# All index keys ahead of the index queries, and tiles 2 to 4 admitted in one piece

## What is computed

```
z = xn @ w_in
u, q, k, v, qi, ki, wi = jnp.split(z, cuts, axis=-1)
...
s = jnp.einsum('bthd,bsd->bths', qi, ki) * (IDX_DIM ** -0.5)
score = jnp.einsum('bths,bth->bts', jax.nn.relu(s), wi)
score = jnp.where(kpos[None, None, :] <= qpos[None, :, None], score, -jnp.inf)
_, sel = lax.top_k(score, topk)            # topk = 256
...
s = jnp.einsum('btkgd,btnkd->btkgn', qg, ksel) * (HEAD_DIM ** -0.5)
s = jnp.where(valid[:, :, None, None, :], s, -jnp.inf)
p = jax.nn.softmax(s, axis=-1)
o = jnp.einsum('btkgn,btnkd->btkgd', p, vsel)
```

## Time and profile before

| | |
|---|---|
| time, median of 3 runs | 1186.83 us (1186.34 to 1189.43) |
| profiled execution | 1187.31 us, span 1185.5 us, mean granted clock .959 |
| TensorE busy | 1076.1 us (91%) |
| VectorE busy | 563.1 us (47%) |
| ScalarE busy | 414.2 us (35%) |
| GpSimd busy | 232.7 us (20%) |

### The profile page before, as it was taken

The page is one execution under the profiler, slowest core; times in us unless marked ns, Lnnn a source line. Parts: engine busy times, 40 slices in busy tenths (PEclk is TensorE's granted clock), DMA queues, the critical chain, the costliest instruction groups (busy, mean ns, idle before and its releaser), DMA issues. The chain is left out here.

```text
span 1185.5 us, 16400 instructions
## 1 busy us (share of the span) xinstructions
PE 1076.1 (91%) x6212; PEld 731.3 (62%) x6212; DVE 563.1 (47%) x1275; ACT 414.2 (35%) x976; POOL 232.7 (20%) x270
## 2 busy tenths in 40 slices
PE   4999999999996888999999898599999999999980
PEld 2555443454453666777788556378787878787860
DVE  3124568999998777766851362212211111111114
ACT  1234446667644244455562234211111111111114
POOL 1433134554420000000040210012121212122110
PEclk9999999999996899999999899789999999999995
DMA  6510000010082211101111752399999999999928
GB/s 222 204 47 12 6 28 1 1 36 6 27 227 76 107 54 54 54 19 54 37 54 63 285 230 72 129 336 356 313 345 338 344 329 347 332 341 341 290 31 311
DMA packets 51198, 191.42 MB, mean 161 GB/s; under 512 B 10910, under 2 KB 13806, under 8 KB 40885
## 3 DMA queue, kind: packets, MB, share of 16 engines
q1 hardware_dynamic: 39439, 142.71, 34.0%
q0 software_dynamic: 11536, 47.71, 14.2%
q10 hardware_dynamic: 158, 0.16, 0.1%
HBM read 162.49 MB, written 28.19 MB: 161 GB/s over the span
## 5 line engine op out<-in xcount | busy, mean ns | idle before, releaser
L1500 PEld LDWEIGHTS ps<-mem 128*128 128x128 f32 x2048 | 236.9, 194 | 16.7 <-issue 16.7
L1576 ACT ACTIVATE mem<-ps 128x512 f32<-128x512 f32 (+8 forms) x342 | 150.8, 484 | 247.1 <-PE ps L1298 63.0
L1500 PE MATMUL ps<-mem 128*128 128x96 f32 x2048 | 236.3, 277 | 0.8 <-DVE mem L2481 0.8
L2049 DVE TENSOR_SCALAR_CACHE_REDUCE mem<-mem 128x768 bf16<-128x768 f32 (+2 forms) x134 | 166.5, 1283 | 0.0
L1341 PE MATMUL ps<-mem 128*128 128x256 f32 (+1 forms) x544 | 126.3, 385 | 4.5 <-DVE mem L2347 3.5
L1506 PE MATMUL ps<-mem 128*96 128x512 f32 x256 | 117.6, 602 | 2.5 <-DVE mem L2473 2.5
L1341 PEld LDWEIGHTS ps<-mem 128*128 128x128 f32 (+1 forms) x544 | 100.6, 190 | 20.8 <-DVE mem L2347 5.6
L2473 DVE TENSOR_TENSOR mem<-mem,ps 128x192 f32<-128x192 f32 x32 | 11.4, 355 | 213.2 <-ACT mem L1925 213.2
L1002 POOL DMA_INDIRECT h_rows<-mem x32 | 46.5, 1454 | 296.4 <-DVE mem L2488 287.2
L1925 ACT ACTIVATE mem<-ps 128x192 f32<-128x192 f32 x32 | 10.6, 332 | 262.8 <-PE ps L1500 262.8
L1506 PEld LDWEIGHTS ps<-mem 128*96 128x96 f32 x256 | 39.1, 162 | 57.1 <-issue 51.2
(11 more groups left out here) (303 smaller groups left out, 1396.1 us busy)
## 6 DMA issues: line engine op xcount, KB each, us to landing
mem<-in_expert_w_gate SPq DMA_DIRECT2D x32, 1024.0 KB, 5.2
mem<-in_expert_w_up SPq DMA_DIRECT2D x32, 1024.0 KB, 8.8
mem<-in_expert_w_down SPq DMA_DIRECT2D x32, 1024.0 KB, 13.3
mem<-in_x_prompt SPq DMA_DIRECT2D x16, 512.0 KB, 4.1
mem<-in_w_in SPq DMA_DIRECT2D x3, 2048.0 KB, 10.9
h_rows<-mem SPq DMA_DIRECT2D x8, 512.0 KB, 2.6
xn_rows<-mem SPq DMA_DIRECT2D x8, 512.0 KB, 2.8
mem<-h_rows SPq DMA_DIRECT2D x8, 512.0 KB, 5.9
```

Of the source, the lines that this page charges most:

```text
L1500: ins = mm(ps[:, 2 + s, j * CAP:(j + 1) * CAP], wgu[w][:, j // 2, k, (j % 2) * P:(j % 2 + 1) * P], xgT[:, s, k, :], start=(k == 0), stop=( ...
L1576: return fn(out, in_, ACT.Copy, scale=scale)
L2049: v.tensor_scalar(bufs[a % 3][0:R, 0:w], sc, mid[:, a:a + 1], None, ALU.is_ge, ALU.add, accum_out=cnt[:, a:a + 1]).then_inc(step, 1)
```

## The change

There are two parts. In phase 1 the keys of all nine tiles come first, then the index queries, in the order `ASKING = [7, 6, 5, 4, 3, 2, NT]`; those of tiles 0 and 1, which no selection reads, are left out. And the admission of tiles 2 to 4 is done by VectorE in one piece ahead of the copies of the samples' scores, not in phase 2b; `PIECES` stays as it is.

```diff
+ASKING = [7, 6, 5, 4, 3, 2, NT]
...
         order = [("T0", ("x", 0)), ("T1", ("x", 0))]
-        score_steps = {}
-        m = 0
-        for n in range(TILES + 1):
-            if n < TILES:
-                order += [("B5", ("KV", n))]
+        for n in range(TILES):
+            order += [("B5", ("KV", n))]
             if n + 1 < TILES:
                 order += [("T0", ("x", n + 1)), ("T1", ("x", n + 1))]
             if n:
-                order += [("T1", ("qi", n - 1)), ("T0", ("k", n - 1))]
-                i = ORDER[n - 1]
-                score_steps[n - 1] = []
-                if 2 <= i < NT:
-                    for lo in range(0, P * (i + 1), 512):
-                        for h in range(NH):
-                            score_steps[n - 1].append((m, lo, min(512, P * (i + 1) - lo), h))
-                            order += [(f"S{m % 4}", ("s", m))]
-                            m += 1
-            if n < TILES:
-                order += [("B4", ("QI", n))]
+                order += [("T0", ("k", n - 1))]
+        order += [("T0", ("k", TILES - 1))]
+        score_steps = {}
+        m = 0
+        for n, i in enumerate(ASKING):
+            order += [("B4", ("QI", n)), ("T1", ("qi", n))]
+            score_steps[n] = []
+            if i < NT:
+                for lo in range(0, P * (i + 1), 512):
+                    for h in range(NH):
+                        score_steps[n].append((m, lo, min(512, P * (i + 1) - lo), h))
+                        order += [(f"S{m % 4}", ("s", m))]
+                        m += 1
```

TensorE's loop. The keys' turn and the index queries' turn are functions of their own now (`k_turn`, `qi_turn`; each waits for `z_ready` of GpSimd and claims T0 or T1):

```diff
                 keys_values(n)
                 if n + 1 < TILES:
                     x_turn(n + 1)
-                between = scores(n - 1) if n else nothing
+                if n:
+                    k_turn(n - 1)
+            index_queries(0, nothing)
+            k_turn(TILES - 1)
+            index_queries(1, nothing)
+            qi_turn(0)
+            for n in range(2, len(ASKING)):
+                between = scores(n - 2)
                 index_queries(n, between)
                 for _ in between:
                     pass
+                qi_turn(n - 1)
...
-            between = scores(TILES - 1)
+            between = scores(len(ASKING) - 2)
             for n in range(TILES):
                 pool_inputs(n, between)
...
+                if n == 0:
+                    qi_turn(len(ASKING) - 1)
```

SyncE asks for the index queries' weights (2 MB) behind the rows of the fifth tile, and for the next weights and the samples' index weights behind all rows. GpSimd's `rope` becomes two functions:

```diff
+            def rope_keys(n):
...
+                link(turn_halves(z[:, 0:3, :], 3, i, r))
+                pool.tensor_copy(z[:, 3, :], z[:, 2, :]).then_inc(z_ready, 1)
                 if n:
                     pool.wait_ge(kv_out, 48 * n)
...
+            def rope_index_queries(n):
...
             for n in range(TILES):
-                rope(n)
+                rope_keys(n)
...
+            for n in range(len(ASKING)):
+                rope_index_queries(n)
```

ScalarE's slots for the coarse rounds:

```diff
             for n in range(TILES):
                 keep_u(n)
-                some_rounds(n)
                 if n:
+                    some_rounds(n)
                     keep_q(n - 1)
                     some_rounds(n)
                 keep_queries(n)
+                if n == 0:
+                    keep_qi(len(ASKING) - 1)
...
-                some_rounds(n)
                 if n:
+                    some_rounds(n)
                     keep_pool(n - 1)
                     some_rounds(n)
```

VectorE:

```diff
-            for n in range(TILES + 1):
-                if n + 2 < TILES:
-                    norm(n + 2)
-                if n and score_steps[n - 1]:
-                    add_scores(n - 1)
-                    if ORDER[n - 1] == NEAR[-1] + 1:
-                        run(bound(near, 0))
-                        ask_coarse(0)
+            for n in range(TILES - 2):
+                norm(n + 2)
                 if n + 3 < TILES:
                     sum_squares(n + 3)
+            for n, i in enumerate(ASKING[0:6]):
+                add_scores(n)
+                if i == NEAR[-1]:
+                    run(bound(far, 3))
+                if i in NEAR[0:2]:
+                    halvings(far, 3, 2)
+            run(bound(near, 0))
+            ask_coarse(0)
             dve.drain().then_inc(phase1, 1)
-            run(bound(far, 3))
-            halvings(far, 3, ITERS)
+            halvings(far, 3, ITERS - 4)
             admit_group(far, 3)
             take_coarse(0)
             halvings(near, 0, FINE)
+            admit_group(near, 0)
+            dve.nop().then_inc(masks_ready, 1)
...
-            near_admitted = []
-
             def selections():
-                unhalve(near, 0)
-                for a, entry in enumerate(near):
-                    yield from admit(entry, a)
-                dve.nop().then_inc(masks_ready, 1)
-                near_admitted.append(True)
                 yield from select([(SCs[0:SR, :], LS, SR, const("tailmask", SR), None, (sJ, sG, sT))], 6, sample_step, admitted)
```

More of the change, by code:

```diff
@@ L852, in rope @@
                 pool.dma_start(rowsof(k_rows, i), z[:, 0:2, :].rearrange("p a d -> p (a d)")).then_inc(kv_out, 16)
-                pool.dma_start(rowsof(ik_rows, i), z[:, 10, :]).then_inc(kv_out, 16)
+                pool.dma_start(rowsof(ik_rows, i), z[:, 2, :]).then_inc(kv_out, 16)
                 pool.dma_start(rowsof(v_rows, i), V[0:r, i, :]).then_inc(kv_out, 16)
+            def rope_index_queries(n):
+                i = ASKING[n]
+                r = rows(i)
+                z = Z[0:r, n % 2, 4:12, :]
+                copied(pool, "1", "B4", ("QI", n))
+                if i < NT:
+                    turn_halves(z, NH, i, r).then_inc(z_ready, 1)
+                    pool.wait_ge(z_ready, TILES + n + 1)
+                    return
+                link(turn_halves(z, NH, i, r))
+                link(pool.tensor_copy(Ztwice[0:r, :, 0, :], z))
+                pool.tensor_copy(Ztwice[0:r, :, 1, :], z).then_inc(z_ready, 1)
             def rope_q(n):
@@ L926, in _ @@
                     pool.wait_ge(kv_out, 48 * TILES)
-                    take(pool, "1", "T1", ("qi", TILES - 1))
+                    take(pool, "1", "T1", ("qi", len(ASKING) - 1))
                     take(pool, "1", "T0", ("k", TILES - 1))
@@ L1080, in keys_values, with k_turn, qi_turn @@
                 ins.then_inc(filled["1B5"], 1)
-            def z_turn(n):
-                i = ORDER[n]
+            def k_turn(n):
+                r = rows(ORDER[n])
+                z = Z[0:r, n % 2]
+                pe.wait_ge(z_ready, n + 1)
+                claim(pe, "1", "T0", ("k", n))
+                for c in range(2):
+                    ins = tr(ps[:, 0, c * r:(c + 1) * r], z[:, 2 * c:2 * c + 2, :].rearrange("p a d -> p (a d)"), ident(r))
+                ins.then_inc(filled["1T0"], 1)
+            def qi_turn(n):
+                i = ASKING[n]
                 r = rows(i)
                 z = Z[0:r, n % 2]
-                pe.wait_ge(z_ready, n + 1)
+                pe.wait_ge(z_ready, TILES + n + 1)
                 claim(pe, "1", "T1", ("qi", n))
@@ L1117, in index_queries @@
             def index_queries(n, between):
-                r = rows(ORDER[n])
-                tok = slice(ORDER[n] * P, ORDER[n] * P + r)
+                i = ASKING[n]
+                r = rows(i)
+                tok = slice(i * P, i * P + r)
                 if n == 0:
@@ L1602, in keep_keys_values @@
                 copy(z[:, 0:2, :].rearrange("p a d -> p (a d)"), kv[:, 0:P])
-                copy(z[:, 10, :], kv[:, 2 * P:2 * P + HD])
+                copy(z[:, 2, :], kv[:, 2 * P:2 * P + HD])
                 copy(V[0:r, i, :], kv[:, P:2 * P])
@@ L1625, in keep_z, with keep_k @@
                     copy(qiT[:, i % 2], four(ps[:, 1, :], r)).then_inc(emptied["1T1"], 1)
+            def keep_k(n):
+                i = ORDER[n]
+                r = rows(i)
+                tok = slice(i * P, i * P + r)
                 take(act, "1", "T0", ("k", n))
@@ L1721, in _ @@
                 if n:
-                    keep_z(n - 1)
-                    relus(score_steps[n - 1][0:12])
-                keep_index_queries(n)
-                if n:
-                    relus(score_steps[n - 1][12:])
+                    keep_k(n - 1)
                 if n + 3 < TILES:
                     root(n + 3)
-            keep_z(TILES - 1)
-            relus(score_steps[TILES - 1])
+            keep_index_queries(0)
+            keep_k(TILES - 1)
+            keep_index_queries(1)
+            keep_qi(0)
+            for n in range(2, len(ASKING)):
+                relus(score_steps[n - 2][0:12])
+                keep_index_queries(n)
+                relus(score_steps[n - 2][12:])
+                keep_qi(n - 1)
+            relus(score_steps[len(ASKING) - 2])
             between = coarse()
```

64 lines of the change are left out of this document (24 added, 40 removed).

## The result

The changed kernel took 1201.40 us (median of 4 runs, 1198.33 to 1203.55) against 1186.59 (4 runs, 1185.25 to 1189.43): ratio 1.0123, 95% interval 1.0103 to 1.0144. The forecast was 1188 with a range to 1196, so it was wrong: the loss is small, but the interval lies wholly above 1. Run again beside later kernels, unaltered, it took 1198.40 against 1186.84: 1.0097 (1.0069 to 1.0125). The profiled execution took 1198.33 us, span 1196.5, 11.0 more than the span before.

A forecast was written before the change was run, and what follows sets the result against it. TensorE was taken as nearly full up to the experts, limited by its waits and clock. Barrier -3.0, tiles 0 and 1 +4.3, tiles 2 and 3 -8.3, tile 6 +8.3 sum to +1.3: 1188 us, range 1181 to 1196.

The forecast's parts named there:

- The barrier: Start of phase 2b's first chunk, set by VectorE: 361.3 against 364.28, -3.0 us, bounds -4.5 to +6.
- the rest ends near 310: VectorE's remaining far work before the barrier ends near 310; it then waits for ScalarE's coarse rounds until 318.3.
- Tiles 2 and 3: Phase 2b: TensorE's waits on VectorE shrink or go, with half-clock matmuls behind them, -8.3 us (-10 to +3).
- Tiles 0 and 1: Phase 2b: the samples' longer pieces start 18 pieces earlier and delay TensorE, +4.3 us (0 to 7).
- Tile 6: Phase 2b: four pieces of the samples' admission in one slot, a wait of 6.6 plus 1.7 half clock, +8.3 us.
- The stalls on VectorE: Phase 1: far work ahead of tile 3's and 2's adds holds TensorE up, 3.1 and 3.3, +6.3 us.
- One: Rival, slower: phase 2b pays and does not gain, waits in tiles 2 and 3 only move; 1194 us, chance .17.
- Two: Rival, slower: the key phase is paced by stores, three tiles late by 2.8; 1196 us, chance .07.
- three: Rival, slower: the clock falls in the key phase, 2.2 more eight times; 1206 us, chance .04.
- Four: Rival, faster: samples' admission hidden in tile 6, 1180 us, or tiles 0 and 1 cost nothing, 1184; chance .13.
- five: Rival, faster: phase 1's bubbles and stalls are covered, TensorE 15 earlier, -11 at the barrier; 1180 us, chance .11.
- Six: Rival: no gain before the barrier, since 14.5 of admission eat all; 1191 us, chance .11.

The follow-up runs named there:

- far_short: Changed kernel with two of the halvings of tiles 5 to 7 left out (20 and not 22): 1193.38 us, ratio 1.0056.
- adm_only: Kernel before, old phase 1 kept, with only the admission of tiles 2 to 4 moved ahead of the samples' scores: 1209.61 us, ratio 1.0184.
- skip18: Changed kernel with the first 18 pieces of phase 2b left empty, so the samples' selection starts where it did before: 1190.88 us, ratio 1.0021.
- after_table: Changed kernel with the table of pieces refitted, none in tiles 0 and 1: 1181.15 us, ratio .9946.
- p1_dense: p1_only with the samples' first key copies ahead of the last five coarse steps and the key phase's gaps taken out: 1177.27 us, ratio .9916.
- p1_only: Changed kernel's new phase 1, with the admission of tiles 2 to 4 put back among phase 2b's pieces: 1182.99 us, ratio .9956.
- best2: p1_dense with tile 2 admitted ahead of the samples' scores and a fitted table of pieces: 1170.73 us, ratio .9877.
- best3: best2 with the samples' bounds and first count one by one in tile 1, and a refitted tile 6: 1168.18 us, ratio .9829.
- p1_table: p1_only with the table of pieces refitted from tile 2 on, entries of tiles 0 and 1 kept: 1183.21 us, ratio .9966.

## Why the prediction was wrong

**The barrier, -3.0 forecast, +2.0 measured (+3.5 from the same start, so 1.5 of the miss was hidden by an earlier start, which I had not forecast).** The step that failed is "the rest ends near 310". VectorE's 22 far halvings begin at 204.16, not at some 193: the near bound and the asking for the coarse rounds, 10.5 us, stand behind the adds as well, and I had them nowhere. From the turn, the near bound also starts 2.0 later than the far bound did before, and the halvings and the far admission take 1.6 more. Far work thus ends at 323.07, and "VectorE waits for it [the coarse rounds]" was false. The rounds themselves were well placed (316.7 against 318.3, and 292.6 against 292.7 from the turn), as were the near halvings (28.6 for 28.5) and the admission (14.6 for 14.5). I also took it that VectorE had room among the adds. After tile 4's adds, at 156.49, its row has no gap: far work put ahead of the last adds only made these adds later. `far_short` shows what was right in it: some 6 us under the changed kernel the rounds do take over.

**Tiles 2 and 3, -8.3 forecast, -3.1 measured (-5.4 in the second profile).** The waits were right, and each new one is where it was put: forecast 1.1, 2.1, 2.3 and 2.0, measured .98, 1.69, 1.83 and 1.73. With .86, .65 and .15 that I had at nothing they are 7.9 in all, forecast 7.5, before 12.3. The term that was mis-sized is the clock. I counted 3.5 of half-clock time (1.7, 1.6 and .2) as gained with the long waits. It came back behind the short ones: L1367 takes 4.19 at 436.52 and 4.42 at 449.71 (3.62 at full clock), and the groups from 434 to 454 together are about 4.9 over their length at full clock, where the two such stretches before, at 409 and from 433 to 440, were about 3.4. So 4.4 was gained in waits and 1.3 given back.

The two terms missed by 5.0 and 5.2. The sum missed the profiled span by 9.9 (11.2 against 1.3); the rest are -.5 in tiles 0 and 1, -.8 in tile 4 and +1.0 behind it.

**What was right.** Tiles 0 and 1 (+4.3, +3.8): S(1, 0) came 15.5 behind S(0, 0), forecast 16, behind a minimum, a maximum and two counts, of which I had one. Tile 6 (+8.3, +9.3), the wait to .1, the half clock behind it 3.0 and not 1.7. The key phase's period; and the seven coarse steps ahead of the samples' keys, though they cost 3.9 and not 2.4. The stalls on VectorE were 2.2 and not 6.3; that the index queries between the scores cover more than the buffers do is my reading, no run isolates it. It changed nothing at the barrier, because TensorE waits there for VectorE.

**The rivals.** One (phase 2b pays and does not gain) came nearest in number, with "the -8.3 shrinks to -3 or less", but not by what it said: the waits did shrink, and the clock took the gain. It was also priced without the barrier's error, which I had bounded by stalls only. Two and three did not occur: TensorE had no wait for stores, and the clock was 1.00 through the key phase, gaps of .47 and all. The Trainium skill's page "TensorE: Matmul & The Clock Gate", section "A second HAM failure mode: psum-queue depth-cycling", has it that small idle gaps between groups of matmuls make the clock swing; in the key phase this trace does not show it. Four and five did not occur. Six said that there would be no gain before the barrier, and there was none, +2.0 for its 0; the admission cost the 14.5 that it named, but behind it stood the late far work too.

**What caused the loss**, as shown: 2.0 at the barrier (3.5 less 1.5 of an earlier start) and 3.8 + 9.3 in slots that the old table overfilled, less 3.9 in tiles 2 to 4. `adm_only` has the losses in phase 2b without the new phase 1, and in `skip18`, where only the shift of the pieces is undone, tiles 0 and 1 and the wait in tile 6 are back at the times of before or below. With the table refitted the same change is faster than before (`after_table`), and without its second part faster still once phase 1 is tightened (`p1_dense`).

## What to carry to other kernels

Take away work from a list that another table deals out by number, and everything behind it changes its slot: refit the table in the same edit, so that no slot holds two long pieces. When an engine takes work from behind a barrier to before it, add up that engine's row from its last fixed point to the barrier, every small group included, and only then ask what it waits for. A gap on an engine that waits at the barrier can still cost: first look whether the row of the engine that comes last starts behind it, as VectorE's row starts behind the adds that TensorE paces. And compare two traces from an early landmark, not from the start of the span: here the start alone moved every later time by up to 2 us, while the barrier lay 344.10 to 344.22 behind that landmark in all four programs with the same phases.

## What the runs showed of the hardware that was not expected

The same wait of 2.4 us between the same instructions was followed by full clock in one program and by half clock in another that differs only ahead of the barrier (2.38 at 468.48 before, 2.39 at 464.34 in `p1_only`); tile 3 takes 35.9 or 38.7 us by it. Even two runs of one program differ: behind the wait of 1.69 in tile 2 of the changed kernel the granted clock from 432 to 436 was .78 in the first profile and 1.00 in the second. Gaps of .47 and less, two a tile over 50 us, left the granted clock at 1.00. In the two fastest kernels (`best2`, `best3`) the mean clock was .963 and .962, in the slowest (`adm_only`) .951. The first keys' 16 matmuls took 5.89 (`p1_table`) to 7.36 us (`after_table`) in programs that are the same up to there.
